# Joining the output projection and the expert routing of a hybrid diffusion step into one block

## The reference

```python
mix = concat(mla, hgrn, rwkv)                       # (640, 1024)
x   = layernorm(ALPHA * x + g1 * (mix @ w_out)) * ln_g + ln_b
h   = x * (1 + sc2) + sh2                           # per feature, one pair for each token group
aff = softmax(h @ router, axis=-1)                  # router (1024, 16)
gate, idx = top_k(aff.T, cap)                       # 64 of 512 sample and 16 of 128 context tokens per expert
xe  = h[idx]
he  = silu(xe @ w1) * (xe @ w3);  ye = (he @ w2) * gate
y   = zeros.at[idx].add(ye)
x   = layernorm(ALPHA * x + g2 * y) * ln_g2 + ln_b2
```

## Time and profile before

| what | us |
|---|---|
| median of 3 runs | 2893.16 (2885.23 to 2896.66) |
| profiled execution, its own time | 2892.97 |
| its span in the trace | 2891.2 |
| output products to the first refill, layer 0 | 762.8 to 897.8 |
| share of the span in which TensorE is busy | 86% |

### The profile page before, as it was taken

The page is one execution under the profiler, slowest core; times in us unless marked ns, Lnnn a source line. Parts: engine busy times, 40 slices in busy tenths (PEclk is TensorE's granted clock), DMA queues, the critical chain, the costliest instruction groups (busy, mean ns, idle before and its releaser), DMA issues. The chain is left out here.

```text
span 2891.2 us, 76516 instructions
## 1 busy us (share of the span) xinstructions
PE 2492.4 (86%) x34482; PEld 1738.0 (60%) x34482; DVE 1200.2 (42%) x2514; ACT 550.5 (19%) x1174; POOL 614.4 (21%) x754
## 2 busy tenths in 40 slices
PE   6999989798866999999779999887988479999994
PEld 3576545596445666666346765556863366666662
DVE  3477846545342121111254877564453411111213
ACT  2111533221110010000131134332221101000101
POOL 1254500233130000000142535003221300000002
PEclk9999999999978999999899999999999689999997
DMA  7011000104646999999730011001145379999994
GB/s 291 8 43 39 14 30 1 64 26 179 247 161 229 396 400 393 393 398 408 278 142 25 26 41 41 1 1 64 49 189 228 146 284 395 394 396 392 398 387 162
DMA packets 76605, 560.85 MB, mean 194 GB/s; under 512 B 14024, under 2 KB 15880, under 8 KB 37368
## 3 DMA queue, kind: packets, MB, share of 16 engines
q1 hardware_dynamic: 70136, 534.97, 46.6%
q0 software_dynamic: 6144, 20.98, 3.1%
HBM read 528.78 MB, written 27.13 MB: 192 GB/s over the span
## 5 line engine op out<-in xcount | busy, mean ns | idle before, releaser
L2661 PE MATMUL ps<-arena 128*64 128x80 f32 x16384 | 614.0, 235 | 63.4 <-issue 58.7
L2661 PEld LDWEIGHTS ps<-arena 128*64 128x64 f32 x16384 | 587.6, 138 | 111.2 <-issue 108.5
L2757 DVE TENSOR_TENSOR arena<-arena,ps 128x160 f32<-128x160 f32 x128 | 41.2, 322 | 651.6 <-ACT arena L2710 651.6
L2675 PE MATMUL ps<-arena 128*64 128x512 f32 x1024 | 256.1, 610 | 10.4 <-issue 5.3
L2710 ACT ACTIVATE arena<-ps 128x160 f32<-128x160 f32 x128 | 38.9, 304 | 847.3 <-PE ps L2661 847.3
L735 PE MATMUL ps<-arena,x_sb 128*128 128x512 f32 (+1 forms) x704 | 194.7, 435 | 3.5 <-ACT arena L924 1.9
L2418 POOL DMA_INDIRECT sum_d<-arena x32 | 45.6, 1426 | 648.3 <-DVEq L2750 648.3
L735 PEld LDWEIGHTS ps<-arena,x_sb 128*128 128x128 f32 x704 | 107.9, 191 | 89.3 <-issue 84.2
L1859 POOL TENSOR_TENSOR arena<-arena,rwl_sb 128x512 f32<-128x512 f32 x50 | 64.1, 1289 | 413.8 <-ACT arena L1801 344.3
L2679 PE MATMUL ps<-arena 128*16 128x256 f32 x2048 | 136.4, 382 | 0.0
L2412 POOL DMA_INDIRECT arena<-h_d,arena x32 | 40.3, 1258 | 419.9 <-DVEq L2728 352.2
(11 more groups left out here) (361 smaller groups left out, 3982.1 us busy)
## 6 DMA issues: line engine op xcount, KB each, us to landing
arena<-in_ex_w SPq DMA_DIRECT2D x128, 2048.0 KB, 16.2
arena<-in_ex_w SPq DMA_DIRECT2D x128, 1024.0 KB
arena<-in_ada_w SPq DMA_DIRECT2D x32, 1024.0 KB, 6.9
arena<-in_ada_w SPq DMA_DIRECT2D x8, 2048.0 KB, 21.1
x_sb<-in_w_t SPq DMA_DIRECT2D x22, 512.0 KB, 4.2
arena<-in_w_t SPq DMA_DIRECT2D x12, 512.0 KB, 6.6
x_sb<-in_x SPq DMA_DIRECT2D x2, 2560.0 KB, 16.1
h_d<-x_sb SPq DMA_DIRECT2D x10, 512.0 KB, 2.6
```

What stands on the lines that cost most here:

```text
L2661: m = nc.tensor.matmul(gated(j)[c * 64:(c + 1) * 64, f, a, :], w13[q % WG][:, a, k, f * P + c * 64:f * P + (c + 1) * 64], xT[:, x % 2, k, ...
L2675: nc.tensor.matmul(sample_out(x, h), he[:, x % 2, f, 0:CAPS], w2[:, q % WP, f % 2, h * 512:(h + 1) * 512], start=f == 0, stop=f == KD - 1)
```

## The change

Both phases become one block. `hT` stays at its place (over `mixT`, of which each tile's columns are free once its products are done), the small route buffers move behind the output weights. TensorE makes the products of tiles 0 to 3, turns tiles 0 and 1, makes the products of tile 4, and then turns and router products alternate as tiles become ready. The router products are made in two 64-column tiles. ScalarE and VectorE share the modulated columns in a written-out order; the last tile's norm weight and bias go from GpSimd to VectorE; ALPHA goes from GpSimd to ScalarE. The sixth w13 block is loaded once the indices stand.

```diff
 def norm_steps(...):
-    def scalar(act):
-        for t in range(TILES):
+    def scalar(act, t):
...
     def pool(pl, c):
-        for t in range(TILES):
+        for t in range(TILES - 1):
...
+    def turned(n):
+        return ps[:, (1, 5, 2, 6, 3, 7, 1, 5, 2, 6)[n], :]
...
         def _(sp):
             load_gate_rows(e, sp, 0, brow, S["n1ld"])
             load_norm_rows(e, sp, 0, gb, S["n1ld"])
+            sp.dma_start(rt, d["router"][l]).then_inc(S["ld_rt"], 16)
+            sp.dma_start(base, d["base"]).then_inc(S["ld_rt"], 16)
             e.clear_last(sp)
             for q in range(WG - 1):
                 load_w13(e, sp, q, mem)
             for t in range(TILES):
-                sp.wait_ge(S["n1x"], t + 1)
+                if t < LAST:
+                    sp.wait_ge(S["n1x"], t + 1)
+                else:
+                    sp.wait_ge(S["n1y"], 1)
                 sp.dma_start(e.h2_d[t * P:(t + 1) * P, :], e.x[:, t, :]).then_inc(S["st_x"], 16)
-            sp.wait_ge(S["st_x"], 16 * TILES)
+            for q in range(WP):
+                load_w2(e, sp, q, mem)
+            for t in range(TILES):
+                sp.wait_ge(S["x_al"], t + 1)
+                sp.dma_start(e.sum_d[t * P:(t + 1) * P, :], e.x[:, t, :]).then_inc(S["st_sum"], 16)
+            sp.wait_ge(S["iu"], 1)
+            load_w13(e, sp, WG - 1, mem)
+            sp.wait_ge(S["st_sum"], 16 * TILES)
...
+            def turn(t):
+                for n in (2 * t, 2 * t + 1):
+                    for k in range(4):
+                        kk = 4 * (n % 2) + k
+                        m = nc.tensor.transpose(turned(n)[:, k * P:(k + 1) * P], e.x[:, t, kk * P:(kk + 1) * P], e.ident[:, :])
+                    m.then_inc(S["rx_ps"], 1)
+            def logits(t):
+                for k in range(KD):
+                    for c in range(2):
+                        m = nc.tensor.matmul(ps[c * 64:(c + 1) * 64, 0, t * NE:(t + 1) * NE], hT[:, k, t * P + c * 64:t * P + (c + 1) * 64],
+                                             rt[:, k, :], start=k == 0, stop=k == KD - 1)
+                return m
+            for t in range(4):
+                products(t)
+            pe.wait_ge(S["op_ev"], 2)
+            pe.wait_ge(S["n1x"], 1)
+            turn(0)
+            pe.wait_ge(S["op_ev"], 3)
+            pe.wait_ge(S["n1x"], 2)
+            turn(1)
+            products(4)
+            pe.wait_ge(S["op_ev"], 4)
+            pe.wait_ge(S["n1x"], 3)
+            turn(2)
+            pe.wait_ge(S["ld_rt"], 32)
+            pe.wait_ge(S["op_ev"], 5)
+            pe.wait_ge(S["rx_act"], 4)
+            logits(0)
+            logits(1)
+            pe.wait_ge(S["n1x"], 4)
+            turn(3)
+            pe.wait_ge(S["rx_act"], 6)
+            logits(2)
+            pe.wait_ge(S["rx_act"], 7)
+            pe.wait_ge(S["rx_dve"], 1)
+            logits(3)
+            pe.wait_ge(S["n1y"], 1)
+            turn(4)
+            pe.wait_ge(S["rx_act"], 8)
+            pe.wait_ge(S["rx_dve"], 2)
+            logits(4).then_inc(S["lg_ps"], 1)
...
+        def _(act):                       
+            for t in range(3):
+                scalar(act, t)
+            columns(0)
+            columns(1)
+            scalar(act, 3)
+            for n in range(2, 6):
+                columns(n)
+            scalar(act, 4)
+            columns(6)
+            columns(8)
+            act.wait_ge(S["lg_c"], 1)
+            nc.scalar.activation(lg, lg, ACT.Exp).then_inc(S["lg_e"], 1)
+            act.wait_ge(S["st_x"], 16 * TILES)
+            act.wait_ge(S["rx_ps"], 2 * TILES)
+            for t in range(TILES):
+                nc.scalar.activation(e.x[:, t, :], e.x[:, t, :], ACT.Copy, scale=ALPHA).then_inc(S["x_al"], 1)
...
             vector(dve, v)
+            columns(7)
+            dve.wait_ge(S["n1xn"], TILES)
+            v.link(nc.vector.tensor_tensor(e.x[:, LAST, :], e.x[:, LAST, :], gb[:, 0, :], ALU.mult))
+            nc.vector.tensor_tensor(e.x[:, LAST, :], e.x[:, LAST, :], gb[:, 1, :], ALU.add).then_inc(S["n1y"], 1)
+            columns(9)
...
+            pl.wait_ge(S["st_x"], 16 * TILES)
+            pl.wait_ge(S["iu"], 1)
+            for x in range(2):
+                gather_tokens(e, x, mem)
```

More of the change, by code:

```diff
@@ new lines, in _, with columns @@
+            m.then_inc(S["af_ps"], 1)
+            pe.wait_ge(S["top"], 1)
+            nc.tensor.transpose(ps[0:CAP, 3, 0:NE], pf, e.ident[0:NE, 0:NE])
+            nc.tensor.transpose(ps[0:CAP, 3, NE:2 * NE], val, e.ident[0:NE, 0:NE]).then_inc(S["ti_ps"], 1)
+        @block.scalar
+        def _(act):
+            def columns(n):
+                t, b = divmod(n, 2)
+                g = 1 if t else 0
+                act.wait_ge(S["rx_ps"], n + 1)
+                for k in range(4):
+                    kk = 4 * b + k
+                    m = nc.scalar.activation(hT[:, kk, t * P:(t + 1) * P], turned(n)[:, k * P:(k + 1) * P], ACT.Identity,
+                                             bias=e.modc[:, g, 3, kk:kk + 1], scale=e.modc[:, g, 4, kk:kk + 1])
+                m.then_inc(S["rx_act"], 1)
+            for t in range(3):
[12 more added lines that the diff above has]
+            act.wait_ge(S["rx_ps"], 2 * TILES)
+            for t in range(TILES):
+                nc.scalar.activation(e.x[:, t, :], e.x[:, t, :], ACT.Copy, scale=ALPHA).then_inc(S["x_al"], 1)
@@ L2359, in _, with columns @@
             v = e.chain("dve", dve)
-            vector(dve, v)
+            def columns(n):
+                t, b = divmod(n, 2)
+                g = 1 if t else 0
+                dve.wait_ge(S["rx_ps"], n + 1)
+                for k in range(4):
+                    kk = 4 * b + k
+                    m = nc.vector.tensor_scalar(hT[:, kk, t * P:(t + 1) * P], turned(n)[:, k * P:(k + 1) * P],
+                                                e.modc[:, g, 4, kk:kk + 1], e.modc[:, g, 3, kk:kk + 1], ALU.mult, ALU.add)
+                m.then_inc(S["rx_dve"], 1)
@@ new lines, in _ @@
+            vector(dve, v)
+            columns(7)
[3 more added lines that the diff above has]
+            columns(9)
+            dve.wait_ge(S["lg_ps"], 1)
+            v.link(nc.vector.tensor_copy(lg, ps[:, 0, 0:TILES * NE].rearrange("p (a b) -> p a b", a=TILES)))
+            m3 = mx.rearrange("p (n o) -> p n o", o=1).to_broadcast([P, TILES, NE])
@@ new lines, in _ @@
+            for c0, c1, k0, k1 in ((NPR, NTOK, 0, CAPS), (0, NPR, CAPS, CAP)):
+                for k in range(k0, k1, 8):
+                    v.link(nc.vector.max(val[:, k:k + 8], aT[:, c0:c1]))
+                    v.link(nc.vector.max_index(pos[:, k:k + 8], val[:, k:k + 8], aT[:, c0:c1]))
+                    if k + 8 < k1:
+                        v.link(nc.vector.match_replace(aT[:, c0:c1], val[:, k:k + 8], aT[:, c0:c1], -1.0))
+            v.link(nc.vector.tensor_copy(pf, pos))
+            dve.wait_ge(S["ld_rt"], 32)
@@ L2361, in _ @@
+            v.link(nc.vector.tensor_tensor(pf, pf, base, ALU.add))
+            dve.sem_inc(S["top"], 1)
+            dve.wait_ge(S["ti_ps"], 1)
+            nc.vector.tensor_copy(iu, ps[0:CAP, 3, 0:NE]).then_inc(S["iu"], 1)
+            v.link(nc.vector.tensor_copy(gv, ps[0:CAP, 3, NE:2 * NE]))
             e.done("dve", v)
-        @block.scalar
-        def _(act):
-            scalar(act)
         @block.gpsimd
@@ L2436, in load_w2 @@
                  ).then_inc(e.S[f"ld_f{q % WP}"], 16)
[L2439 to L2551, removed]
-                    v.link(nc.vector.max(val[:, k:k + 8], aT[:, c0:c1]))
-                    v.link(nc.vector.max_index(pos[:, k:k + 8], val[:, k:k + 8], aT[:, c0:c1]))
-                    if k + 8 < k1:
-                        v.link(nc.vector.match_replace(aT[:, c0:c1], val[:, k:k + 8], aT[:, c0:c1], -1.0))
-            v.link(nc.vector.tensor_copy(pf, pos))
-            dve.wait_ge(S["ld_rt"], 32)
-            v.link(nc.vector.tensor_tensor(pf, pf, base, ALU.add))
-            dve.sem_inc(S["top"], 1)
-            dve.wait_ge(S["ti_ps"], 1)
-            nc.vector.tensor_copy(iu, ps[0:CAP, 3, 0:NE]).then_inc(S["iu"], 1)
-            v.link(nc.vector.tensor_copy(gv, ps[0:CAP, 3, NE:2 * NE]))
-            e.done("dve", v)
```

42 lines of the change are left out of this document (32 added, 10 removed).

## The result

| | before | after |
|---|---|---|
| median, us | 2889.19 (4 runs, 2880.80 to 2896.66) | 2854.16 (4 runs, 2851.08 to 2859.62) |
| ratio after / before | | 0.987, 95% interval 0.9849 to 0.9891 |
| profiled execution, us | 2892.97 | 2851.54 |

The forecast was 2855.6 us, with a range of 2842 to 2869. The time came out 35.0 us lower by the medians and 41.4 by the two profiled executions; the experiments show which of these is the change.

The account below looks back on a forecast made before the run. The expert stage was taken as a fixed-length weight stream started by the first refill, behind one serial chain. 2892.97 - 42.8 (earlier logits, both layers) + 5.4 (gathers beside the weight block) = 2855.6 us, range 2842 to 2869.

Parts of the forecast that it names:

- The bound: Expert stage is a weight stream of fixed length; the gain is how much earlier its first refill comes in each layer.
- Turning ahead: Tiles 0 and 1 turned before the last tile's products: 1.65 us plus 0.2 us of hand-overs added before the norm.
- The norm and the two routes: Last norm stays 6.39 us with turns and logits beside it; then two parallel paths lead to turn 4.
- route (a): After the last normalisation ScalarE moves its half of tile 3, TensorE makes logits 3; ends 829.8 at half clock, sets turn 4.
- route (b): VectorE moves its half of tile 3, then multiplies and adds for the last tile in GpSimd's place; ends at 828.8.
- The tail: Turn 4, its columns and logits 4 at half clock: logits copied at 835.3 instead of 856.25; 42.8 us over both layers.
- rival 1: Full clock through to the logits' copy: 2.8 us less in each layer, 2850 us; chance 0.15.
- Mode of the array: Switching TensorE between 64-column products and whole transposes shows no visible drain, so no cost was put in the sum.
- ALPHA: Five ScalarE copies of 1.24 us lie beside VectorE's top-k; sum_d stores land by 857, 3 us to spare.
- The gathers: Sixth w13 block sets out with the two gathers and delays the block's end: 2.7 us a layer, bounds 0 and 6.1.
- rival 2: Gathers pay fully for the weight block beside them, 6.1 us instead of 2.7, or sum_d stores equally late: 2862.4; chance 0.15.
- rival 5: Slower: gathers starve behind the late weight block, needing over 21 us for each pair; past 2907 us; chance 0.02.

Follow-up runs that it names:

- e6: The changed kernel with tile 4's products right after tile 3's and turns 0 and 1 behind them: 2862.16 us (1 run).
- e5: The changed kernel with the last tile's norm weight and bias on GpSimd again: 2858.24 us (1 run).
- e2: The kernel before with only the router products made in two 64-column tiles: 2874.71 us, ratio 0.9934 to before.
- e1: The changed kernel with the router products in whole 128-column weights again: 2873.84 us, ratio 0.9932 to before.
- e3: The changed kernel with the sixth w13 block issued only after both gathers have landed: 2844.65 us, ratio 0.9845 to before.
- e7: The changed kernel with the multiplication by ALPHA on GpSimd again, after the last h2 store: 2858.70 us (1 run).

## Why the prediction was right, point by point

*The bound.* Right. The first refill decides: the sum of E fell by 35.2 us and the median by 35.0. The stream behind it, from first refill to the loads of the sums, is 533.7 and 527.1 us before and 537.1 and 524.9 after, with no common sign.

*Turning ahead.* Forecast 1.85 us; A grew by 1.74 in layer 0 and 0.94 in layer 1. Without it (e6) A and B together are 6 us longer.

*The norm and the two routes.* Right by their order and nearly by their times: from the eviction to the end of ScalarE's normalisation it is 6.39 us again, route (a) ends at 830.69 and route (b) at 829.93, and turn 4 follows route (a). e5 shows the 0.7 us between them.

*The tail.* Forecast 17.4 us from where the eviction was before, measured 16.9 in layer 0 and 16.1 in layer 1: a narrow record at half clock costs 59 ns and not 66, which is 0.4 us over two tiles' logits, and in layer 1 the turning ahead added 0.9 us less than forecast. The gain to the logits is 44.7 us (21.5 and 23.2), 42.8 were forecast. That the clock is at half in logits 3 and 4 was right; rival 1 is out. The prediction called the router products the largest piece of the gain, 14.7 us a layer that come back as 2.1. Taken apart, the narrow weights alone shorten E by 8.3 us a layer (e2) and the joining alone by 11.2 (e1), so the narrowing is the smaller part.

*Mode of the array.* No drain can be seen: turn 3 ends at 825.47 and the narrow logits 2 start at 825.41. The gap of 0.61 us ahead of logits 0 isn't one either, since it is 0.61 in e1 too, where the logits have whole weights. The rival behind which the prediction put the Trainium skill's rule (TensorEngine Tiling, Key Properties) is out in this case.

*ALPHA.* Right: it lies beside the top-k. The sum_d stores landed in 7.7 to 8.9 us, long before the indices, and nothing waited for them.

*The gathers.* This is the term that was mis-sized. The place, the mechanism and the bounds (0 to 6.1) hold, but the price is 4.6 us in layer 0 and 5.4 in layer 1, 10.0 together and not 5.4. The step that failed is "the gathers, sharing, somewhat before the block's last piece": they don't share from the start but move mostly behind it, and land in 8.6 us in place of 4.2 (e3). The price was close to rival 2's (6.1 a layer, chance 0.15). 0.6 us of it is GpSimd's late issue, for which the prediction had no term.

*The signs.* Two of those that the prediction named did not come. The copy of the logits was to come 17 to 18 us after the last eviction begins, and it came after 15.1. That was a slip of reference: the prediction's own times, 835.3 and 819.75, are 15.55 apart, and 17.4 counts from the eviction of before. The next block was to start 8 to 9.5 us after the first gather's issue, and it started 10.1 and 10.7 after it, which is the mis-sized term. The two vector operations (1.22 and 1.23 us) and the logits records (1.90 us at half clock) came as named. In rival 5, 21 us for each pair would only use up the gain; to pass 2907 takes about 28.7.

*The total.* 44.7 less 10.0, and 0.5 from a first refill that came sooner after the block's start, which is within what that stretch moves from run to run, make 35.2. The forecast of 37.4 had one term 1.9 us too small and one 4.6 us too small, which cancel in part. That the profiled execution came out 4 us below the forecast, though 2 us less were won than forecast, is owed to S as well, 8.7 us shorter by chance. The median's closeness to the forecast, 1.4 us, is luck in part for the same reason: the forecast starts from an execution 3.8 us above the median of before.

## What to carry to other kernels

A block's end that waits for small gathers makes a bulk load issued just ahead of them dear: send the bulk load earlier or behind their landing, and keep in the block only the gather that the next one needs first. When a serial tail is cut into pieces that hide beside a norm, check whether every piece still fits after its neighbours, since one that slips puts all later ones in line. Judge an edit of some microseconds by the stretches that it touches; stretches with the same code moved by up to 10 us from one execution to the next.

## What the runs showed of the hardware that was not expected

- With a 2 MB weight block issued 0.9 us ahead of a gather, none of the gather's packets moved for the first 4.0 us after its issue (1.5 us when alone), and its landing took 8.6 us in place of 4.2.
- GpSimd issued the first gather 0.47 us after the indices' copy where ALPHA was its last work before (14 us back in e7, 33 us in the kernel before), and 1.08 to 1.09 us after it where the norm was (31 us back in e5, 44 us in the changed kernel). So the length of the idle time doesn't decide it; what does isn't seen.
- After the last output products the granted clock stayed at full through the turns, the narrow logits 0 to 2 and the wait behind them, to 828.7, and was at half in logits 3. With whole-width logits 0 and 1 in their place (e1), its mean was 0.74 from 824.6 to 826.7, and turn 3 at 826.71 already ran at half, 1.95 us against 1.09.
